# The first modulation by pairs of k-tiles, with three chunks of w_in beside it

## The chip, the cores and the metric

One core of a Trainium2 chip (trn2). The metric is the device time of one execution in microseconds; the times before are three runs of the same kernel.

## The reference, cut to what matters

Two transformer blocks on x of 256 tokens and 2048 channels, all in FP32. What the change touches is the start of the first block:

```python
mod = jax.nn.silu(c) @ w_ada[l] + b_ada[l]
shift1, scale1, gate1, shift2, scale2, gate2 = jnp.split(mod, N_MOD, axis=-1)
h = rms_norm(x, norm1_w[l]) * (1.0 + scale1[:, None]) + shift1[:, None]
proj = h @ w_in[l]
u_pool, q, k, v, g_a, g_b = jnp.split(proj, split_at, axis=-1)
```

c is one row of 2048, w_ada is 2048 x 12288, w_in is 2048 x 8192. Behind it come the pooling and the stick-breaking attention on u_pool, q, k and v, two up-projections under the gates g_a and g_b, w_o, the feed-forward (w_ff1, w_ff2), and a second pair of mixers (a: banded attention, b: compressed attention) with a final norm.

## The kernel before, in words

All five engines have a program written out by hand, in the order in which it runs; semaphores alone tie them together (`Marks`). TensorE multiplies 128 x 128 tiles of activations, turned (`act_a_high` and `act_a_low`, k-tile by k-tile), with chunks of 512 weight columns. Weights and activations are split into a high and a low part (fp32r), and a product is three matmuls (`mm_tile`, lines 571 to 573) for each of the two token tiles; so one k-tile of a chunk is six matmuls of 512 columns, and a chunk of 16 k-tiles is 96.

The weights come as a stream (`weight_stream`): SyncE (SP) loads units of four k-tiles, 1 MB each, into the ring `raw` of four (line 421); ScalarE (ACT) casts half a unit, two k-tiles, to `w_high` (1013), VectorE (DVE) makes `w_low` from the difference (1446), both three halves ahead of TensorE in rings of four. SP waits for the `w_low` of the unit that a load overwrites. Each chunk is finished before the next begins, in one of two pairs of PSUM banks. The order is "in" 0 to 7 (the first quarter, the fourth, the second, the third of the four parts of 1024, twice), "ga" and "ua" four times each in turn, "gb" and "ub" the same, "wo", and the rest.

Ahead of it stands a prologue. The shift and the scale of the first norm are 4096 columns of `c @ w_ada`. SP loads them as 32 pieces of four k-tiles by 512 columns into `raw` (404). Of the four k-tiles TensorE takes one as a product of a single row (615), DVE two as running sums in `ada_acc_vec` (1510, 1514), GpSimd (POOL) one in `ada_acc_pool` (463 to 468); the two sums are folded into the row by matmuls with ones (618, 620), ACT copies the row out of PSUM (1043), and TensorE turns it into columns (623). In the middle, after four of eight column groups, stand the transposes of the normalised x (582), copied by DVE (1524). When all columns are there, DVE makes `mod1` (1529, 1531), and ACT and DVE modulate and split two k-tiles at a time into `act_a_high` and `act_a_low` (1050, 1053, 1536).

The other 32 pieces of w_ada, of 256 columns, are spread over later chunks (`PIECES`): POOL loads them in ring buffers of two k-tiles (438), DVE sums 16 k-tiles, one instruction each (1464, 1467), TensorE adds up over the partitions (591, 599), DVE keeps the result. Eight pieces lie in "in", four in "ga", eight in "gb" and "ub", four in "wo", eight in "f1". In "ga" and "ua" DVE also works for the stick-breaking attention: at the start of each ga it copies `k_pair` and `v_pair` (1642, 1643), for which the scores on TensorE wait (697, at k = 2), and at the end of each ua it multiplies the gate in (1661). In chunk 1 of "in" DVE and POOL also make the counts and bands of the pooling; chunks 2, 3, 6 and 7 end with a normalisation of the heads on DVE (up to 1585).

Of the kernel before, what the change touches and what calls it, by code (L numbers as in the profile page):

```python
# [38 lines left out]
PRO = 2 * D // CH * (KT // UK)  # L39
# [7 lines left out]
                 "cols_made", "c_tanh", "x_squared", "xn_made", "row_copied", "xT_made", "ident_made"),  # L47
# [53 lines left out]
class Chunk:  # L101
    def __init__(self, w, row, col, nk, half, unit, pair, width, before, k0, whole):
        self.w, self.row, self.col, self.nk = w, row, col, nk
        self.k0, self.first, self.last = k0, k0 == 0, k0 + nk == whole
        self.half, self.unit, self.pair, self.width, self.before = half, unit, pair, width, before
        self.per = SK if width == CH else KT // 2
        self.halves = nk // self.per


def weight_stream(t):  # L110

    chunks, every = {}, []
    state = {"half": 0, "unit": 0}
    newest = {0: None, 1: None}

    def add(name, w, row, col, nk, pair, width=CH, k0=0, whole=None):
        c = Chunk(w, row, col, nk, state["half"], state["unit"], pair, width, newest[pair], k0, whole or nk)
        c.name = name
        state["half"] += c.halves
        state["unit"] += c.halves // 2  # L120
        newest[pair] = c
        chunks[name] = c
        every.append(c)

# [8 lines left out]
    for i in range(2):  # L133
        add(("in", 4 * i), w_in, 0, CH * i, KT, 0)
        add(("in", 4 * i + 1), w_in, 0, 3 * POOL_W + CH * i, KT, 1)
        add(("in", 4 * i + 2), w_in, 0, POOL_W + CH * i, KT, 0)
        add(("in", 4 * i + 3), w_in, 0, 2 * POOL_W + CH * i, KT, 1)
# [32 lines left out]
    return chunks, every, state["half"]  # L170
# [3 lines left out]
PIECES = ([(("in", n), 2 * D + AC * n) for n in range(8)]  # L174
          + [(("ga", n), 3 * D + AC * n) for n in range(4)]
          + [((("gb", "ub")[j], n), 3 * D + AC * (4 + 2 * n + j)) for n in range(4) for j in range(2)]
          + [(("wo", n), 3 * D + AC * (12 + n)) for n in range(4)]
          + [(("f1", i, 2 * j), 5 * D + AC * (2 * i + j)) for i in range(4) for j in range(2)])
PIECE_OF = {name: p for p, (name, _) in enumerate(PIECES)}

# [35 lines left out]
def body(nc, t, ctx, known):  # L216
    m = Marks(nc, ctx, known)
    landed, of = m.landed, m.of
    C, EVERY, HALVES = weight_stream(t)
# [5 lines left out]
    pair = [banks[:, 0:2, :], banks[:, 2:4, :]]  # L225
# [34 lines left out]
    acc_g = sb("ada_acc_pool", [P, 2, CH], 121984)  # L260
    row_s = sb("ada_row", [1, 2, CH], 126080)
# [167 lines left out]
    def pool_program(G):  # L429
# [24 lines left out]
        for w in range(PRO):  # L454
# [1653 lines left out]
```

## Time and profile before

| | |
|---|---|
| three runs | 2411.17, 2414.98, 2419.09 us (median 2414.98) |
| the profiled execution | 2406.36 us, span 2405.1 us, mean granted clock 0.969 |
| busy share of PE, PEld, DVE, ACT, POOL | 94%, 75%, 64%, 45%, 12% |
| chain that ended last | PE 86%, DVE 7%, DMA 2%, ACT 2%, issue 2% |
| DMA | 468.52 MB, mean 195 GB/s |

PE is TensorE at its matmuls, PEld at its weight loads, which overlap them. The span runs from the first to the last instruction of the profiled execution, and is 1.3 us shorter than its time. The chain is followed back from the last instruction through whatever released it; its shares say on which engine the time that sets the end was spent. Busy shares are means over stages that differ: the 40 slices of the page show PE at 5 and 7 tenths in the first two (120 us) and at 8 or 9 in almost all later ones. The granted clock is that of TensorE, 1.00 being 2.4 GHz and 0.50 being 1.2 GHz.

### The profile page before, as it was taken

To read this page: it belongs to the slowest core of one execution; us is meant where nothing else is said; L and a number is where in the kernel's file an instruction comes from. 1 tells how busy PE (TensorE), PEld (TensorE's weight loads), DVE (VectorE), ACT (ScalarE), POOL (GpSimd) and SP (SyncE) were. 2 spreads that over 40 slices of the span, in tenths; PEclk is the share of its full clock that TensorE was granted. 3 is DMA by queue.
4 is the path that set the end of the run, shared out by engine and by line. 5 is a ranking of instruction groups with operands and counts; after the bars stand their busy time and mean duration, and the time that the engine had idled before them with its cause. 6 is when DMAs were issued, how large, how long until landed. Compare 5 with 4: busy or idle time off the path is not lost.

```text
span 2405.1 us, 27296 instructions
## 1 busy us (share of the span) xinstructions
PE 2253.9 (94%) x10579; PEld 1803.2 (75%) x10579; DVE 1528.9 (64%) x2050; ACT 1084.0 (45%) x1566; POOL 297.4 (12%) x374
## 2 busy tenths in 40 slices
PE   5789999999898999999999998999998879999998
PEld 1267878877687888888888886788887767877776
DVE  6878778878877645645655655565654435676664
ACT  1054445643346543543543545555545413555543
POOL 6633221123322100100100000000000000000000
PEclk9899999999999999999999999999999989999999
DMA  9887856678877756756756654444446433333333
GB/s 333 291 282 267 279 182 220 214 226 276 265 251 244 231 192 211 237 192 208 236 187 215 222 175 158 158 141 149 149 145 205 136 110 123 123 99 112 106 123 123
DMA packets 225268, 468.52 MB, mean 195 GB/s; under 512 B 13850, under 2 KB 19188, under 8 KB 224500
## 3 DMA queue, kind: packets, MB, share of 16 engines
q1 hardware_dynamic: 196944, 388.78, 48.6%
q0 software_dynamic: 20480, 67.13, 8.6%
q10 hardware_dynamic: 7716, 10.88, 1.3%
q8 instruction: 84, 1.38, 0.2%
q14 instruction: 44, 0.36, 0.0%
HBM read 464.65 MB, written 2.10 MB: 194 GB/s over the span
## 4 chain that ended last, share of the span: by engine, by line
PE 86%; DVE 7%; DMA 2%; ACT 2%; issue 2%; POOL 0%; ACTq 0%; DVEq 0%
PE banks L571 25%; PE banks L573 24%; PE banks L572 24%; PE banks L582 2%; DVE ada_acc_vec L1514 2%; PE banks L832 2%; PE banks L844 1%; DMA ada_w<-in_w_ada 1%; DVE ada_acc L1467 1%; PE banks L858 1%; PE banks L859 1%; PE banks L857 1%; PE banks L922 1%; DMA raw<-in_w_ada 1%; DMA x<-in_x 0%
## 5 line engine op out<-in xcount | busy, mean ns | idle before, releaser
L1446 DVE TENSOR_TENSOR w_low<-raw,w_high 128x1024 fp32r<-128x1024 f32 x674 | 821.6, 1224 | 597.4 <-ACT w_high L1013 596.3
L1013 ACT CAST w_high<-raw 128x1024 fp32r<-128x1024 f32 x674 | 701.2, 1047 | 798.5 <-PE banks L573 797.7
L571 PE MATMUL banks<-w_high,act_a_high 128*128 128x512 f32 (+1 forms) x1696 | 686.5, 405 | 14.3 <-DVE w_low L1446 8.4
L573 PE MATMUL banks<-w_high,act_a_low 128*128 128x512 f32 (+1 forms) x1696 | 665.6, 392 | 0.0
L572 PE MATMUL banks<-w_low,act_a_high 128*128 128x512 f32 (+1 forms) x1696 | 664.6, 392 | 0.0
L571 PEld LDWEIGHTS banks<-w_high,act_a_high 128*128 128x128 f32 x1696 | 324.9, 192 | 92.4 <-issue 22.0
L573 PEld LDWEIGHTS banks<-w_high,act_a_low 128*128 128x128 f32 x1696 | 323.8, 191 | 69.2
L572 PEld LDWEIGHTS banks<-w_low,act_a_high 128*128 128x128 f32 x1696 | 325.0, 192 | 61.8
L438 POOL DMA_DIRECT2D ada_w<-in_w_ada x256 | 186.8, 730 | 953.4 <-DVE ada_acc L1467 947.2
L571 PE MATMUL banks<-w_high,act_b_high 128*128 128x512 f32 x640 | 250.6, 392 | 0.8 <-DVE act_b_low L1671 0.8
L573 PE MATMUL banks<-w_high,act_b_low 128*128 128x512 f32 x640 | 249.6, 390 | 0.0
L572 PE MATMUL banks<-w_low,act_b_high 128*128 128x512 f32 x640 | 249.6, 390 | 0.0
L1467 DVE SCALAR_TENSOR_TENSOR ada_acc<-ada_w,cT,ada_acc 128x256 f32<-128x256 f32 x480 | 231.8, 483 | 16.8 <-DMA ada_w<-in_w_ada 7.5
L571 PEld LDWEIGHTS banks<-w_high,act_b_high 128*128 128x128 f32 x640 | 120.5, 188 | 25.6 <-DVE act_b_low L1671 0.8
L573 PEld LDWEIGHTS banks<-w_high,act_b_low 128*128 128x128 f32 x640 | 120.6, 188 | 25.2
L572 PEld LDWEIGHTS banks<-w_low,act_b_high 128*128 128x128 f32 x640 | 120.6, 188 | 25.0
L443 POOL TENSOR_TENSOR inverse_rms<-sums_for_rms,minus_half 128x2 f32<-128x2 f32 (+1 forms) x9 | 10.4, 1152 | 976.5 <-DVE sums_for_rms L1485 976.5
L1317 ACT ACTIVATE scores<-scores,minus_max 128x128 f32<-128x128 f32 x192 | 85.1, 447 | 32.5 <-DVE minus_max L1856 30.7
L1514 DVE SCALAR_TENSOR_TENSOR ada_acc_vec<-raw,cT,ada_acc_vec 128x512 f32<-128x512 f32 x56 | 75.2, 1343 | 7.7 <-DMA raw<-in_w_ada 4.4
L1328 ACT COPY ada_w<-banks 128x768 f32<-128x768 f32 x48 | 38.3, 799 | 57.6 <-PE banks L844 57.4
L615 PE MATMUL banks<-raw,cT 128*1 128x512 f32 x64 | 40.2, 762 | 18.4 <-DMA raw<-in_w_ada 13.7
L571 PE MATMUL banks<-w_high,act_d_high 128*128 128x512 f32 x128 | 51.4, 401 | 1.6 <-DVE act_d_low L1671 1.6
(336 smaller groups left out, 2213.9 us busy)
## 6 DMA issues: line engine op xcount, KB each, us to landing
raw<-in_w_ff SPq DMA_DIRECT2D x128, 1024.0 KB, 5.2
raw<-in_w_in SPq DMA_DIRECT2D x64, 1024.0 KB, 6.6
ada_w<-in_w_ada POOLq DMA_DIRECT2D x256, 256.0 KB, 5.0
raw<-in_b_w_in SPq DMA_DIRECT2D x44, 1024.0 KB, 5.0
raw<-in_a_w_in SPq DMA_DIRECT2D x36, 1024.0 KB, 5.1
raw<-in_w_ada SPq DMA_DIRECT2D x32, 1024.0 KB, 7.2
raw<-in_w_o SPq DMA_DIRECT2D x16, 1024.0 KB, 7.3
raw<-in_a_w_out SPq DMA_DIRECT2D x16, 1024.0 KB, 5.2
```

The costliest lines, as they stand in the source:

```text
L438: G.dma_start(ada_w[:, u % ADA_RING, :, :], t["w_ada"][0, q * AK * P:(q + 1) * AK * P, col:col + AC] .rearrange("(k p) n -> p k n", p=P)). ...
L571: T.matmul(out, xh, wh, start=(c.first and k == 0), stop=False)
L572: T.matmul(out, xh, wl, start=False, stop=False)
L573: last = T.matmul(out, xl, wh, start=False, stop=(c.last and k == c.nk - 1))
L582: tr = T.transpose(bank(b)[:, j * SEQ + tt * P:j * SEQ + (tt + 1) * P], src[:, tt, c0 + j * P:c0 + (j + 1) * P], ident[:, :])
L615: T.matmul(row, cT[:, u * UK:u * UK + 1], raw[:, w % RAW, 0, :], start=(u == 0), stop=False).then_inc(*done("pro_pe", w))
L832: mm = T.matmul(bank(e)[:, c0:c0 + n], qG[o:o + HD, i % 4, tt * P:(tt + 1) * P], k_[o:o + HD, 0:n], start=True, stop=True)
L1013: A.copy(WH[:, h % SPL, :, :], split_ap(h)).then_inc(*done("high", h))
L1317: A.activation(sc[:, s, c0:c0 + n], sc[:, s, c0:c0 + n], ACT.Exp, scale=R, bias=nm[:, i // 4, j, tt:tt + 1], accum_out=sm[:, i // 4, j, tt ...
L1446: V.tensor_tensor(WL[:, h % SPL, :, :], split_ap(h), WH[:, h % SPL, :, :].bitcast(F32), ALU.subtract).then_inc(*done("low", h))
L1467: V.scalar_tensor_tensor(out=acc_, in0=w, scalar=c, in1=acc_, op0=ALU.mult, op1=ALU.add).then_inc(*done("ada_acc", (p, a)))
L1514: V.scalar_tensor_tensor(out=acc_v[:, n, :], in0=r[:, kk, :], scalar=cT[:, k + kk:k + kk + 1], in1=acc_v[:, n, :], op0=ALU.mult, op1=ALU.a ...
```

## The change

The modulation of the first norm is made for two k-tiles of the activations at a time, by eight rounds. A round loads the 256 columns of the shift and the 256 of the scale that belong to two k-tiles: four loads of four k-tiles of w_ada, each as two DMAs, into four buffers `ada_first` of their own. Of each buffer DVE sums two k-tiles in `ada_acc_vec`, TensorE takes the other two (half and half) with the weights of w_ada as the stationary operand and one column of c as the moving one, which gives columns at once: 8 matmuls in the program for a buffer, and 4 more that fold in DVE's sum. POOL does none of it. The transposes of x stand after the first round's sums, and their copies are shared between ACT and DVE.

Between the sum groups of the next round stand the matmuls of three chunks of w_in, ("in", 0) to ("in", 2), two k-tiles of each; a third pair of PSUM banks serves the third chunk. Units and halves of these chunks are taken in turn, and SP issues their loads in groups of three between those of w_ada. The pieces of w_ada that lay in "in" 0 to 2 have moved: "in" 3 to 7 take five, each "ua" takes one, "wo" three. The sum over the partitions of a piece always lies in the next chunk (`DUE_STEP`) and in one PSUM bank. The counts and bands of the pooling are made in chunk 3.

```diff
@@ weight_stream
+    cols = [CH * i + part * POOL_W for i in range(2) for part in (0, 3, 1, 2)]
+    early = [define(("in", n), w_in, 0, cols[n], KT, n) for n in range(EARLY)]
+    for i in range(KT // UK):
+        for c in early:
+            take_unit(c, i)
+        for sub in range(2):
+            for c in early:
+                take_half(c, c.units[i], sub)
...
+PLACES = ([("in", n) for n in range(EARLY, 8)] + [(name, n) for n in range(4) for name in ("ga", "ua")]
+          + [(name, n) for n in range(4) for name in ("gb", "ub")] + [("wo", n) for n in range(3)])
+DUE_STEP = {"in": 4, "ga": 5, "ua": 6, "gb": 4, "ub": 4, "wo": 4, "f1": 4}
@@ sync_program
+        def first_load(i, u):
+            if i > 0:
+                S.wait_ge(*of("first_pe", (i - 1, u)))
+                S.wait_ge(*of("first_vec", (i - 1, u, 1)))
+            for m_ in range(2):
+                S.dma_start(first[u][:, :, m_, :], first_w[:, u * UK:(u + 1) * UK, m_, i * AC:(i + 1) * AC]).then_inc(*landed(f"first_landed{u}", i))
...
+        for i in range(KT // 2):
+            for u in range(FIRST_RING):
+                if i % 2 == 0 and u == (2 if i else FIRST_RING):
+                    for n in range(EARLY):
+                        unit_load(i // 2 * EARLY + n)
+                first_load(i, u)
+            if i == 0:
+                for n in range(EARLY):
+                    unit_load(n)
@@ tensor_program
+        def first_pe(i, u):
+            T.wait_ge(*of(f"first_landed{u}", i))
...
+            for kk in (UK - 2, UK - 1):
+                for j in range(4):
+                    mm = T.matmul(sum_cols(i)[:, j:j + 1], first[u][:, kk, j // 2, j % 2 * P:(j % 2 + 1) * P],
+                                  cT[:, u * UK + kk:u * UK + kk + 1], start=(u == 0 and kk == UK - 2 and j == 0), stop=False)
+            mm.then_inc(*done("first_pe", (i, u)))
...
+        for i in range(KT // 2):
+            more = i + 1 < KT // 2
+            for n in range(EARLY):
+                if more:
+                    first_pe(i + 1, n)
+                if n == 0:
+                    T.wait_ge(*of("a_low", ("in", i)))
...
+                for k in (2 * i, 2 * i + 1):
+                    mm_tile(C["in", n], k, STAT["in"])
+            if more:
+                first_pe(i + 1, FIRST_RING - 1)
+                first_sum(i + 1)
@@ vector_program
+        for i in range(KT // 2):
+            more = i + 1 < KT // 2
+            for n in range(EARLY):
+                if more:
+                    first_vec(i + 1, n)
+                if n == 0:
+                    modulate("in", 2 * i, tmp0)
+                    if i == 0:
+                        for h in range(AHEAD):
+                            rest(h)
+                rest(EARLY * i + n + AHEAD)
+            if more:
+                first_vec(i + 1, FIRST_RING - 1)
+                first_mod(i + 1)
...
             for k in range(8):
                 rests(C["ua", n], k)
+                ada_tiles(C["ua", n], k)
+                ada_keep(C["ua", n], k)
```

What PE does in a round stands in its own order of the changed kernel; L638 is a sum group with the weights of w_ada, L645 folds in DVE's sum, and L595 to L597 are the three matmuls of `mm_tile` (each block goes on with nine more like them).

```order
L638 MATMUL banks<-cT,ada_first_77 128x1 [waits columns_vector,first_landed0]
L638 MATMUL banks<-cT,ada_first_77 128x1 x7
L595 MATMUL banks<-w_high,act_a_high 128x512 [waits low_vector,a_low_vector]
...
L638 MATMUL banks<-cT,ada_first_78 128x1 [waits first_landed1]
L638 MATMUL banks<-cT,ada_first_78 128x1 x7
L595 MATMUL banks<-w_high,act_a_high 128x512 [waits low_vector]
...
L638 MATMUL banks<-cT,ada_first_80 128x1 [waits first_landed3]
L638 MATMUL banks<-cT,ada_first_80 128x1 x7
L645 MATMUL banks<-ones,ada_acc_vec 128x1 [waits first_vec_vector]
L645 MATMUL banks<-ones,ada_acc_vec 128x1 x3
```

Before, no matmul of w_in stood on PE ahead of the last column of the modulation; now each block of 12 has a sum group ahead of it, and a round ends with two groups and the fold.

The second place is DVE at the end of the first ua, before the change (1446 is w_low, 1661 the gate, 1642 and 1643 the copies for the next ga):

```order
L1612 TENSOR_SCALAR merged<-merged 128x2x512 [waits pair_scalar]
L1446 TENSOR_TENSOR w_low<-raw,w_high 128x1024 [waits high_scalar] x4
L1661 TENSOR_TENSOR merged<-banks,merged 128x2x512 [waits pair_vector,used_tensor]
L1476 COPY mod_62<-banks 128x2 [waits ada_summed_tensor]
L1642 COPY k_pair<-kT 128x512 [waits stick_tensor]
L1643 COPY v_pair<-values 128x512
```

and of the changed kernel, the same stretch without its middle (1482 is w_low, 1500 and 1503 the sums of a piece of w_ada):

```order
L1666 TENSOR_SCALAR merged<-merged 128x2x512 [waits pair_scalar]
L1482 TENSOR_TENSOR w_low<-raw,w_high 128x1024 [waits high_scalar]
L1500 TENSOR_SCALAR ada_acc<-ada_w,cT 128x256 [waits ada_summed_tensor,ada_landed0]
L1503 SCALAR_TENSOR_TENSOR ada_acc<-ada_w,cT,ada_acc 128x256 [waits ada_acc_vector]
L1503 SCALAR_TENSOR_TENSOR ada_acc<-ada_w,cT,ada_acc 128x256 [waits ada_acc_vector,ada_landed1]
L1503 SCALAR_TENSOR_TENSOR ada_acc<-ada_w,cT,ada_acc 128x256 [waits ada_acc_vector]
L1482 TENSOR_TENSOR w_low<-raw,w_high 128x1024 [waits high_scalar]
...
L1503 SCALAR_TENSOR_TENSOR ada_acc<-ada_w,cT,ada_acc 128x256 [waits ada_acc_vector,ada_landed3]
L1503 SCALAR_TENSOR_TENSOR ada_acc<-ada_w,cT,ada_acc 128x256 [waits ada_acc_vector]
L1718 TENSOR_TENSOR merged<-banks,merged 128x2x512 [waits pair_vector,used_tensor]
L1696 COPY k_pair<-kT 128x512 [waits stick_tensor]
L1697 COPY v_pair<-values 128x512
```

Sixteen sums of a piece have come between the four w_low, all ahead of the gate and the copies.

## Rows read from the trace of the kernel before

**Rows 1.** Windows of the trace; share of DMA engines and GB/s at the right.

```profile
core 0: us, PE busy (x) PEld busy (x) DVE busy (x) ACT busy (x) POOL busy (x), PEclk, DMA share, GB/s
20.00:40.00 20.00, 15.12 (x26) 3.16 (x25) 18.66 (x13) 2.35 (x2) 18.38 (x13) 1.00 0.84 294
...
38.60:45.40 6.80, 5.75 (x18) 1.39 (x16) 4.16 (x4) 0.58 (x1) 2.41 (x4) 1.00 1.03 380
...
80.00:100.00 20.00, 12.16 (x24) 3.08 (x24) 17.58 (x16) 0.93 (x2) 10.80 (x8) 0.74 0.91 319
...
132.80:137.50 4.70, 4.64 (x11) 3.70 (x12) 4.58 (x6) 3.11 (x5) 0.00 (x0) 0.50 1.04 341
```

**Rows 2.** Timeline: start us, us, engine, line; first block matmul, and a cast.

```profile
132.86 0.76 PE L571 MATMUL banks<-w_high,act_a_high 128*128 128x512 f32 x1 [7.12 <-DVE w_low L1446]
...
171.28 1.05 ACT L1013 CAST w_high<-raw 128x1024 fp32r<-128x1024 f32 x1 [1.67 <-PE banks L573]
```

**Rows 3.** Timeline: ACT takes chunks 1 and 2, end of a normalisation on DVE.

```profile
179.68 1.02 ACT L1086 COPY values<-banks 128x1024 f32<-128x1024 f32 x1 [1.91 <-PE banks L573]
...
204.61 1.03 ACT L1091 ACTIVATE qn<-banks 128x1024 f32<-128x1024 f32 x1 [1.61 <-PE banks L573]
...
208.89 1.23 DVE L1585 TENSOR_TENSOR qn<-banks,inverse_rms 128x1024 f32<-128x1024 f32 x1 [1.79 <-POOL inverse_rms L443]
```

**Rows 4.** Timeline of PE: third piece of w_ada, transposes of xn.

```profile
19.31 1.86 PE L615 MATMUL banks<-raw,cT 128*1 128x512 f32 x2 [3.20 <-DMA raw<-in_w_ada]
...
69.63 3.54 PE L582 MATMUL banks<-ident,xn 128*128 128x128 f32 x16 [0.63 <-DVE cols L1521]
...
74.84 1.25 PE L582 MATMUL banks<-ident,xn 128*128 128x128 f32 x8 [0.19 <-DVE xT L1524]
```

**Rows 5.** Timeline of the weight loads (PEld), eight at each clock.

```profile
57.98 1.78 PEld L623 LDWEIGHTS banks<-ones,ada_row 1*128 1x128 f32 x8 [2.45 <-ACT ada_row L1043]
...
41.99 0.96 PEld L623 LDWEIGHTS banks<-ones,ada_row 1*128 1x128 f32 x8 [1.60 <-ACT ada_row L1043]
```

**Rows 6.** Timeline: from the last row turned to the first pair split.

```profile
124.69 1.05 PE L623 MATMUL banks<-ones,ada_row 1*128 1x1 f32 x8 [0.67 <-ACT ada_row L1043]
...
126.27 1.09 ACT L1050 ACTIVATE tmp<-xT,mod 128x256 f32<-128x256 f32 x2 [1.63 <-DVE mod L1531]
...
128.04 0.69 DVE L1536 TENSOR_TENSOR act_a_low<-tmp,act_a_high 128x512 fp32r<-128x512 f32 x1 [1.87 <-ACT act_a_high L1053]
```

**Rows 7.** L1514, the sums of 512 columns on DVE; ns min/median/max.

```profile
L1514 DVE SCALAR_TENSOR_TENSOR ada_acc_vec<-raw,cT,ada_acc_vec x56: 750/1376/1643, 17.3 to 120.5; 128x512 f32<-128x512 f32 x56
```

**Rows 8.** Windows of the trace in mixer b, the chunk of 96 columns.

```profile
1936.40:1939.80 3.40, 3.40 (x31) 3.28 (x29) 1.83 (x7) 2.02 (x3) 0.00 (x0) 1.00 0.62 238
...
1946.70:1950.00 3.30, 3.30 (x17) 3.30 (x17) 0.00 (x0) 0.00 (x0) 0.00 (x0) 0.50 0.02 5
```

**Rows 9.** Window of one period of ga and ua.

```profile
378.40:417.80 39.40, 39.40 (x178) 32.75 (x178) 32.66 (x48) 23.19 (x28) 5.78 (x8) 1.00 0.64 214
```

**Rows 10.** Timeline of DVE and PE around ga and ua.

```profile
385.76 0.69 DVE L1622 TENSOR_TENSOR log_beta<-log_beta,z_log 128x512 f32<-128x512 f32 x1 [0.95 <-ACT z_log L1112]
...
410.92 1.22 DVE L1446 TENSOR_TENSOR w_low<-raw,w_high 128x1024 fp32r<-128x1024 f32 x1
...
419.20 0.42 DVE L1643 COPY v_pair<-values 128x512 f32<-128x512 f32 x1
...
420.68 0.59 PE L697 MATMUL banks<-qT,k_pair 128*128 128x256 f32 x2
```

**Rows 11.** DVE in the first ub (timeline), and its waits, 500 to 660 us.

```profile
527.49 1.23 DVE L1446 TENSOR_TENSOR w_low<-raw,w_high 128x1024 fp32r<-128x1024 f32 x1 [0.24 <-ACT w_high L1013]
...
542.76 1.22 DVE L1690 TENSOR_TENSOR qT<-banks,qT 128x1024 f32<-128x1024 f32 x1
...
DVE ada_acc L1467 <- DMA ada_w<-in_w_ada: 6.8, 4, 2.7
```

**Rows 12.** Waits of PE, 500 to 660 us.

```profile
PE banks L571 <- DVE y_b_low L1665: 4.0, 1, 4.0
```

More of the change, by code:

```diff
@@ L123, in add @@
         every.append(c)
+        return c
+    def add(*args, **more):
+        c = define(*args, **more)
+        for i in range(c.nk // c.per // 2):
+            take_unit(c, i)
+            for sub in range(2):
+                take_half(c, c.units[i], sub)
     def add_outputs(name, w):
@@ L422, in sync_program @@
+        for i in range(KT // 2):
[7 more added lines that the diff above has]
+                    unit_load(n)
+        for u in range(EARLY * (KT // UK), len(UNITS)):
+            unit_load(u)
         for tt in range(NT):
@@ L512, in pool_program @@
             chunk_loads(("ub", n))
-        for n in range(4):
+        for n in range(3):
             chunk_loads(("wo", n))
@@ new lines, in first_sum @@
+        def first_sum(i):
+            T.wait_ge(*of("first_vec", (i, FIRST_RING - 1, 1)))
+            for j in range(4):
+                mm = T.matmul(sum_cols(i)[:, j:j + 1], acc_v[:, i % 2, j * P:(j + 1) * P], ones[:, 0:1],
+                              start=False, stop=(j == 3))
+            mm.then_inc(*done("first_summed", i))
+        emptied[0] = of("c_cols")
+        first_pe(0, 0)
+        first_pe(0, 1)
+        T.wait_ge(*of("small_landed", "rows2"))
+        T.transpose(bank(3)[:, 0:P], rows1[:, :], ident[:, :])
@@ L1069, in heads_store, with first_modulate, in_take @@
                              scale=cols2[:, at[norm]:at[norm] + 1]).then_inc(*done("heads_stored", (n, half)))
-        for n in range(8):
+        def first_modulate(i):
+            A.wait_ge(*of("mod1_made", i))
+            A.wait_ge(*of("xT_made", i))
+            modulate("in", 2 * i, xT[:, 2 * i:2 * i + 2, :], mod1, AH, tmp0)
+        def in_take(n):
+            c = C["in", n]
+            A.wait_ge(*ready(c))
+            if n % 4 == 0:
+                A.copy(u_sb[:, :, CH * (n // 4):CH * (n // 4 + 1)], pair[c.pair]).then_inc(*done("pair_free", c.name))
+            elif n % 4 == 1:
+                if n == 1:
+                    A.wait_ge(*of("a_low", ("in", KT // 2 - 1)))
+                A.copy(vv[:, :, CH * (n // 4):CH * (n // 4 + 1)], pair[c.pair]).then_inc(*done("pair_free", c.name))
+            else:
+                if n > 2:
+                    A.wait_ge(*of("heads_turned", (n - 1 if n % 4 == 3 else n - 3, 1)))
+                A.activation(qn[:, :, :], pair[c.pair], ACT.Square).then_inc(*done("heads_squared", n))
+        first_modulate(0)
+        for h in range(AHEAD):
+            cast(h)
+        for i in range(KT // 2):
+            for n in range(EARLY):
+                cast(EARLY * i + n + AHEAD)
+                if i == KT // 2 - 1 and n > 0:
+                    in_take(n - 1)
+            if i + 1 < KT // 2:
+                first_modulate(i + 1)
+        in_take(EARLY - 1)
+        A.dma_start(wp, t["w_pool"][0].rearrange("g (a q) e -> q (g a) e", q=P)).then_inc(*landed("pool_w_landed"))
+        for n in range(EARLY, 8):
             c = C["in", n]
```

427 lines of the change are left out of this document (179 added, 248 removed).

## The prediction, made before the changed kernel was run

> **What bounds the kernel now.** Read the shares in the table first: TensorE (PE) is busy 94% of a span of 2405.1 us and is 86% of the chain that ended last, so nearly everywhere the end moves with PE's own time. Then the stretches of the opening [rows 1]: in them PE is busy for 12 to 15 of 20 us, mostly with products of a single row that serve the modulation, at a mean granted clock of 0.74 to 1.00. The first block matmul starts only at 132.86 us [rows 2]; TensorE has then still the whole w_in to do. ScalarE (ACT) takes the sums of chunk ("in", 1) at 179.68 and of ("in", 2) at 204.61 us [rows 3]. So I judge the change by two times: when chunk 2 is done, and what the rest costs after it.
>
> **Part 1: the opening up to the first block.** The same bytes arrive in the same order as before (x and four 1 MB pieces of w_ada), so I take the landings of before; the third was used at 19.31 us [rows 4], the fourth landed while its group was at work. A sum group is 8 matmuls in the program, and each FP32 matmul is two weight loads in the trace, so 16 loads; eight such loads took 1.78 us at the lower clock and 0.96 at the upper [rows 5], so a group is 3.6 or 1.9 us. Groups 3 and 4: 19.3 + 3.6 + 3.6 = 26.5; the closing group of 8 loads 1.8, so 28.3. The transposes of xn took 6.5 us (69.63 to 76.1) [rows 4]: 34.8. Then modulation of a pair on ACT (1.09 and the cast), the difference on VectorE (DVE) 0.69 [rows 6], the first w_low 1.2 behind it: **the first block starts at 39 us** instead of 132.9. I cost the splitting of the loads at nothing here, since PE waits for its own groups more than for them.
>
> **Part 2: the eight rounds.** A round has three blocks of 12 matmuls (two k-tiles of each of three chunks), four sum groups and a closing group, all in one row on PE (the first order piece above). A block takes 2.72 us at the upper clock, a cast and its wait for the next, 1.05 + 1.67 [rows 2]. After the closing group PE can start no block until mod1 is added, the pair modulated and split: from the end of L623 (125.74) to the end of act_a_low (128.73) that took 3.0 us [rows 6], and the first group of the next round lies in it. So a round at the upper clock is 3.0 + 3 x 2.72 + 3 x 1.9 + 1.0 = 17.9 us. DVE needs 8 sums of 512 columns at 0.75, the shortest of L1514, when POOL no longer works beside it [rows 7], 0.7 and 3 x 1.22, in all 10.5 us: hidden under PE. ACT needs 3 x 1.05 + 1.7. The DMA brings 4 MiB of w_ada a round and 3 MiB of w_in every second one: 49.3 MB with x and the bias. The busiest stretch shows 380 GB/s, the slowest of those that DMA fills 294 [rows 1], so all of it lies between 130 and 168 us, under the 185 us at which the last round starts; it would bind only where rounds are shorter than they are here.
>
> What decides is the clock. From the third block to the next round's first lie 1.9 + 1.0 + 3.0 = 5.9 us in which PE does nothing but weight loads with one column behind each. The trace has a stretch like it: from 1936.4 us on PE runs loads with 96 columns each (the gates of mixer b) without a gap, first at 1.00, and from 1946.7 us the granted clock reads 0.50 while PE is busy 3.30 of 3.30 us [rows 8]. One column is less than 96, so I expect the clock to fall to 1.2 GHz once in each round, inside that stretch, and to come back in the first block: from 132.8 us dense blocks ran 4.7 us at 0.50 [rows 1], which costs 2.35 us. Another 0.5 us for loads that fall into the lower clock. Between blocks 1, 2 and 3 only one group lies (1.9 us), and I take the clock to stay. Round: 17.9 + 2.35 + 0.5 = **20.8 us**. Seven rounds and the blocks of the eighth: 39 + 7 x 20.8 + 8.2 + 2.35 = 195 us for the end of chunk 2, against 204.6: **9 us gained**. Ends: 173 us with all at the upper clock, 275 with all at the lower (3.6 + 3 x 5.1 + 3 x 3.6 + 1.8 = 31.5 a round).
> By the Trainium skill (TensorE: Matmul & The Clock Gate, "Why this matters for your kernels") it is idle gaps of PE between bursts that cost the upper clock, and here PE would be idle for only about 1.1 us a round, so by that page the clock would stay and the first rival hold; the matmuls of 96 columns speak against it.
>
> **Part 3: chunk 3.** The counts and bands, which lay in chunk 1, now lie in chunk 3, right behind the normalisation of chunk 2 and before that of chunk 3. PE lost about 3 us to what they had put off: 179.68 to 204.61 is 24.9 for 16 k-tiles, where 8 x 2.72 = 21.8. A normalisation keeps DVE 5.5 us from ACT's squares at 204.61 to the end of L1585 at 210.1 [rows 3], and one now lies on either side. I put **3 us** lost (0 to 6).
>
> **Part 4: ga and ua.** There were 24 pieces of w_ada before the feed-forward, 8 in "in"; now "in" takes 5, and the four "ua" chunks take one each (the second order piece). This is the term I trust most. A period of ga and ua lasts 39.4 us, and DVE is busy 32.66 of it [rows 9]. The added piece is 16 instructions at 0.48, about 7.5 us: 40.2, before any wait. And it stands between the w_low of ua and L1661, behind which k_pair and v_pair are copied, for which PE waits at k = 2 of the next ga (L697 at 420.68; the copies end at 419.6, 1.1 us before) [rows 10]. The "ub" chunk has the very sequence: from 527.49 to 542.76, where L1690 starts, 15.3 us, 2.7 of them for a landing of ada_w; the four such waits of the stage are 6.8 us in all [rows 11]. From 410.92 (first w_low of ua) that block now ends not at 417.67 but 12.5 us (no landing wait) to 14.2 (the mean of 1.7) later, at 423.4 to 425.1; L1661 and the copies, 2.0 us; PE would have come at 420.7. The first stall is 4.7 to 6.4 us. In later periods DVE no longer waits for ACT's logarithm (twice 0.95 [rows 10]) nor for a few casts (0.5), so its period is 30.7 (419.6 less 39.4, to 410.92) - 2.4 + 12.5 or 14.2 + 2.0 = 42.8 to 44.5: 3.4 to 5.1 us, twice. At the end y_b_low is late by another 4 to 6, on top of the 4.0 us that PE waits for it already [rows 12]. Sum 16 to 23 us, **20 taken**, since the landing waits came in each of the four ub. The clock lost in these stalls costs nothing extra, DVE being the slower.
>
> **Part 5: the rest.** wo has three pieces instead of four, f1 adds its sums at k = 4 instead of 12; DVE has room there and PE waits for neither: 0. POOL is free until the last round and starts its loads of ada_w only then, ahead of chunk 3 by some 15 us: 0. The row copies on ACT and POOL's accumulator go: they lay in the opening already counted.
>
> **Sum.** -9 + 3 + 20 = +14 us, 2420 against the profiled execution's 2406.4. The median of the runs is 2415.0, 8.6 above that execution; I add the 14 to it: **2429 us**. A measurement of this kernel can tell about 0.3%, 7 us, from no change.
>
> **The rivals.**
> B, the clock stays at 2.4 GHz: chunk 2 ends at 39 + 7 x 17.9 + 8.2 = 173 us, 32 gained, and -32 + 3 + 20 = -9: 2406 us, faster. It decides from rounds under 19 us on. For it: PE does not pause there. Against it: [rows 8]. Chance 0.15.
> C, the clock falls in each gap between blocks too: 17.9 + 3 x 2.35 + 1.5 = 26.5 a round, 240 us for chunk 2, +35 + 3 + 20 = +58: 2473 us; at the lower clock throughout 2508. For it: a mean of 0.74 in an opening whose PE was busy 12 of 20 us [rows 1]. Against it: there PE paused, while from the first block to the third it does not, and dense blocks are most of that time. Chance 0.20.
> D, DVE takes the ua pieces into its idle time (6.7 us of each 39.4) and the stage costs 5 us: -9 + 3 + 5, 2414 us, same. For it: DVE has 6.7 idle and 7.5 come. Against it: 3.3 of the idle time are waits for ACT in the middle of a chain, and the place is the worst one. Chance 0.15.
> The forecast has 0.50; its own range is 2418 to 2440.
>
> **How the numbers follow.** Faster: B's greater part, and the edges of D and of the forecast, 0.18. Same: the rest of B, most of D, the forecast's low end, 0.22. Slower: 0.60. The range begins at 2402 (B with the lower end of part 4) and ends at 2468, which leaves out most of C and little else.
>
> **What would show it.** In the profile after: first block at 39 us; eight rounds of about 21 us; granted clock at 0.50 for some 5 to 8 us of each round, about 0.7 to 0.8 in the mean; chunk 2 taken at about 195 us; PE idle before L697's counterpart for 3 to 6 us in each ga from the second on, released by the pair copies on DVE, and DVE over 95% busy in ga and ua. If the mean clock of the rounds is 0.95 or more, B holds; if a round takes 26 us, C. If PE does not wait for k_pair, part 4 is wrong.

## The result, and the profile after

| | before | after |
|---|---|---|
| median of the runs on one chip | 2413.07 us (2408.37 to 2419.09) | 2444.07 us (2441.02 to 2453.50) |
| ratio, 95% interval | | 1.0139 (1.0115 to 1.0163) |
| profiled execution, mean granted clock | 2406.36 us, 0.969 | 2453.50 us, 0.955 |
| first block matmul | 132.86 us | 40.78 us |
| ACT takes chunk 2, chunk 4 | 204.61, 250.77 | 193.43, 251.50 |
| ga(1), ga(2), ga(3), gb(0) begin | 378.4, 417.8, 457.3, 500.8 | 382.8, 430.8, 479.5, 536.5 |
| xn of the feed-forward begins | 757.1 | 798.3 |

The change costs 31 us of median where 14 were forecast: slower as predicted, inside the range, by twice the size. The profiled execution after is itself 9 us above its median, and that of before lay below its own, so the two traces differ by 47 us; which stage loses is read from the traces, how much in all from the medians. What one pair of traces shows is compared with the traces of the other runs where it can be.

The opening is as forecast. Windows of the trace after: two stretches of 20 us in the rounds, then the end of one round and the first block of the next.

```profile
core 0: us, PE busy (x) PEld busy (x) DVE busy (x) ACT busy (x) POOL busy (x), PEclk, DMA share, GB/s
...
60.00:80.00 20.00, 18.89 (x108) 16.64 (x108) 10.10 (x14) 4.67 (x7) 0.00 (x0) 0.84 0.95 307
80.00:100.00 20.00, 19.14 (x108) 16.86 (x108) 9.79 (x15) 4.44 (x7) 0.00 (x0) 0.84 0.78 267
...
76.20:79.60 3.40, 2.69 (x25) 2.60 (x24) 1.77 (x5) 2.03 (x4) 0.00 (x0) 0.90 0.68 215
79.80:85.60 5.80, 5.54 (x14) 4.40 (x15) 2.84 (x4) 0.42 (x1) 0.00 (x0) 0.50 0.70 227
```

The timeline between them, PE, DVE and ACT:

```profile
76.07 1.03 PE L645 MATMUL banks<-ones,ada_acc_vec 128*128 128x1 f32 x8
76.97 1.93 PE L638 MATMUL banks<-cT,ada_first 128*128 128x1 f32 x16
...
77.54 1.09 ACT L1077 ACTIVATE tmp<-xT,mod 128x256 f32<-128x256 f32 x2 [6.42 <-DVE mod L1560]
...
79.31 0.69 DVE L1581 TENSOR_TENSOR act_a_low<-tmp,act_a_high 128x512 fp32r<-128x512 f32 x1 [0.61 <-ACT act_a_high L1080]
80.06 0.80 PE L595 MATMUL banks<-w_high,act_a_high 128*128 128x512 f32 x1 [1.17 <-DVE act_a_low L1581]
```

Rounds last 20.1 to 20.5 us (the folds begin at 56.00, 76.07, 96.37 and so on to 178.08). The fold, the sum group and the 1.17 us of waiting are followed by a first block wholly at 1.2 GHz (0.50): 12 matmuls in 5.3 us instead of 2.7.

What follows is not as forecast. ACT takes chunks 2, 3 and 4 (timeline after; the last line is chunk 4 before), and PE's waits in chunks 3 and 4:

```profile
193.43 1.03 ACT L1107 ACTIVATE qn<-banks 128x1024 f32<-128x1024 f32 x1 [0.70 <-PE banks L597]
...
220.20 1.03 ACT L1107 ACTIVATE qn<-banks 128x1024 f32<-128x1024 f32 x1 [3.85 <-PE banks L597]
...
251.50 1.02 ACT L1099 COPY merged<-banks 128x1024 f32<-128x1024 f32 x1 [1.61 <-PE banks L597]
...
250.77 1.02 ACT L1082 COPY merged<-banks 128x1024 f32<-128x1024 f32 x1 [1.61 <-PE banks L573]
```

```profile
212.18 0.50 PE L595 MATMUL banks<-w_high,act_a_high 128*128 128x512 f32 x1 [1.15 <-DVE w_low L1482]
...
217.15 0.50 PE L595 MATMUL banks<-w_high,act_a_high 128*128 128x512 f32 x1 [1.93 <-DVE w_low L1482]
...
224.12 0.50 PE L595 MATMUL banks<-w_high,act_a_high 128*128 128x512 f32 x1 [1.24 <-DVE w_low L1482]
...
228.03 0.70 PE L621 MATMUL banks<-ada_acc,ones 128*128 128x256 f32 x2 [0.88 <-DVE ada_acc L1503]
232.37 1.86 PE L606 MATMUL banks<-ident,qn 128*128 128x128 f32 x8 [3.64 <-DVE qn L1621]
```

From chunk 2 to chunk 4 it takes 58.1 us, where before it took 46.2 (from 204.61 [rows 3] to 250.77): the 11.2 us won in the rounds are gone by the end of chunk 4. PE idles 8.8 us in five places, all for DVE, and behind the last of them the clock stood at 0.50 for 3.4 us.

In ga and ua: the waits of PE and of DVE (365 to 705 us) and two windows, the second a whole period:

```profile
PE banks L732 <- DVE v_pair L1697: 18.4, 3, 7.0
PE banks L606 <- DVE qT L1746: 15.5, 4, 8.1
...
DVE ada_acc L1503 <- DMA ada_w<-in_w_ada: 12.6, 8, 2.3
DVE log_beta L1676 <- ACT z_log L1148: 10.7, 6, 2.5
...
PE banks L595 <- DVE y_b_low L1721: 9.3, 1, 9.3
```

```profile
417.70:430.80 13.10, 13.10 (x59) 10.90 (x58) 11.72 (x19) 7.01 (x9) 4.02 (x6) 1.00 0.71 230
...
430.80:479.50 48.70, 41.66 (x182) 34.37 (x182) 40.36 (x65) 23.41 (x27) 11.91 (x17) 0.93 0.68 221
```

Against [rows 9] a period has 9.3 us more; DVE is busy 40.36 us of it, 7.7 more, which is the added piece. It is not over 95% busy, as I had said it would be, but 83%. The three periods of the table grew by 8.6, 9.2 and 13.5 us, 31.3 in all, of which 5.3 is the longer wait for y_b_low at the end (9.3 us for 4.0 [rows 12]).

### The profile page after: what moved, and what is told of

Read it like the earlier page. It is cut to its first block, busy times and chain, and to the rows that moved or that the text cites. A ratio compares the mean times of both kernels' runs of the same rounds, so it can differ in the third digit from the quotient of the medians.

```text
span 2451.9 us, 28078 instructions
## 1 busy us (share of the span) xinstructions
PE 2296.1 (94%) x10995; PEld 1888.1 (77%) x10995; DVE 1491.2 (61%) x2061; ACT 1082.3 (44%) x1562; POOL 218.9 (9%) x318
## 4 chain that ended last, share of the span: by engine, by line
PE 76%; issue 10%; DVE 7%; DMA 3%; ACT 2%; POOL 1%; ACTq 0%; SPq 0%; DVEq 0%; POOLq 0%
PE banks L595 22%; PE banks L597 22%; PE banks L596 22%; PE banks L606 2%; DMA ada_w<-in_w_ada 2%; DVE ada_acc L1503 2%; PE banks L861 2%; PE banks L873 1%; PE banks L888 1%; PE banks L887 1%; PE banks L886 1%; PE banks L951 1%; DMA ada_first<-in_w_ada 1%; DVE w_low L1482 1%; ACT w_high L1043 1%
## 5 line engine op out<-in xcount | busy, mean ns | idle before, releaser
L595 PE MATMUL banks<-w_high,act_a_high 128*128 128x512 f32 (+1 forms) x1696 | 700.3, 413 | 27.4 <-DVE act_a_low L1581 9.7
L597 PE MATMUL banks<-w_high,act_a_low 128*128 128x512 f32 (+1 forms) x1696 | 676.4, 399 | 0.0
L596 PE MATMUL banks<-w_low,act_a_high 128*128 128x512 f32 (+1 forms) x1696 | 675.9, 399 | 0.0
L595 PEld LDWEIGHTS banks<-w_high,act_a_high 128*128 128x128 f32 x1696 | 331.8, 196 | 109.0 <-issue 17.4
L597 PEld LDWEIGHTS banks<-w_high,act_a_low 128*128 128x128 f32 x1696 | 330.8, 195 | 72.1
L596 PEld LDWEIGHTS banks<-w_low,act_a_high 128*128 128x128 f32 x1696 | 332.2, 196 | 63.6
L595 PE MATMUL banks<-w_high,act_b_high 128*128 128x512 f32 x640 | 251.2, 392 | 1.4 <-DVE act_b_low L1727 1.4
L597 PE MATMUL banks<-w_high,act_b_low 128*128 128x512 f32 x640 | 250.1, 391 | 0.0
L595 PEld LDWEIGHTS banks<-w_high,act_b_high 128*128 128x128 f32 x640 | 120.8, 189 | 26.5 <-DVE act_b_low L1727 1.8
L597 PEld LDWEIGHTS banks<-w_high,act_b_low 128*128 128x128 f32 x640 | 120.8, 189 | 25.5
L483 POOL TENSOR_TENSOR inverse_rms<-sums_for_rms,minus_half 128x2 f32<-128x2 f32 (+1 forms) x9 | 10.6, 1178 | 1163.8 <-DVE sums_for_rms L1525 1163.8
L1353 ACT ACTIVATE scores<-scores,minus_max 128x128 f32<-128x128 f32 x192 | 85.1, 446 | 31.4 <-DVE minus_max L1903 30.7
L638 PEld LDWEIGHTS banks<-cT,ada_first 128*128 128x128 f32 x512 | 70.4, 215 | 12.3 <-issue 8.0
L638 PE MATMUL banks<-cT,ada_first 128*128 128x1 f32 x512 | 67.9, 263 | 9.8 <-DMA ada_first<-in_w_ada 9.8
L595 PE MATMUL banks<-w_high,act_d_high 128*128 128x512 f32 x128 | 51.3, 401 | 1.6 <-DVE act_d_low L1727 1.6
```

Of the source, the lines that this page charges most:

```text
L595: T.matmul(out, xh, wh, start=(c.first and k == 0), stop=False)
L596: T.matmul(out, xh, wl, start=False, stop=False)
L597: last = T.matmul(out, xl, wh, start=False, stop=(c.last and k == c.nk - 1))
L638: mm = T.matmul(sum_cols(i)[:, j:j + 1], first[u][:, kk, j // 2, j % 2 * P:(j % 2 + 1) * P], cT[:, u * UK + kk:u * UK + kk + 1], start=(u ...
L1353: A.activation(sc[:, s, c0:c0 + n], sc[:, s, c0:c0 + n], ACT.Exp, scale=R, bias=nm[:, i // 4, j, tt:tt + 1], accum_out=sm[:, i // 4, j, tt ...
```

## The experiments

All ratios are against the kernel before, on the same chip; gains are told against the changed kernel's 2444.07 us (ratio 1.0139) unless said otherwise. The runs were made on several chips, on which the kernel before had medians of 2410.0 to 2413.1 us, so a gain in these medians is good to some 3 us; the ratios are the safer comparison.

### The ua pieces left out

```diff
-PLACES = ([("in", n) for n in range(EARLY, 8)] + [(name, n) for n in range(4) for name in ("ga", "ua")]
+PLACES = ([("in", n) for n in range(EARLY, 8)] + [(name, n) for n in range(4) for name in ("ga",)]
...
-            if 8 <= p < 24:
+            if 8 <= p < 20:
```

> The four pieces of w_ada in ua are left out with their loads, sums and folds; the modulation of the feed-forward lacks its last four pieces (1024 columns of the scale, taken as zero ahead of the one that is added), so the output is not the reference's. All else is as in the changed kernel. Theory A: the whole excess of ga and ua is theirs; the three periods fall back to 39.4, 39.4 and 43.6 us, and the kernel is faster by 31 us (27 to 35). Theory B: a part of it comes from the sums that now lie in the next chunk (DUE_STEP) and from the loads of ada_w behind them: 10 us or more stay, and it is faster by 15 to 22.

Measured: 2414.98 us, ratio 1.001 (0.9995 to 1.0026), 29 us gained, 31 by the ratios. A window of it as long as a period; y_b_low is awaited 4.3 us again:

```profile
413.40:452.80 39.40, 39.40 (x176) 32.75 (x176) 32.99 (x47) 23.27 (x28) 5.79 (x8) 1.00 0.63 214
```

The scores of one ga and of the next stand 39.3 us apart, where before it was 39.4. So theory A: the pieces in ua are worth 29 to 31 us, not the 20 I had taken, and everything else in the change comes out at about zero.

### Order or load in ga and ua

k_pair ahead of ua's sums:

```diff
-            V.tensor_copy(kS[:, :, :], kT[:, h0:h0 + 2, :])
+            if n == 0:
+                V.tensor_copy(kS[:, :, :], kT[:, h0:h0 + 2, :]).then_inc(*done("pair_copied", (n, "k")))
...
             gate(C["ga", n], m_)
+            if n < 3:
+                V.wait_ge(*of("sb_scored", (n, 1)))
+                V.tensor_copy(kS[:, :, :], kT[:, h0 + 2:h0 + 4, :]).then_inc(*done("pair_copied", (n + 1, "k")))
             for k in range(8):
```

> The copy k_pair for the next ga is taken ahead of the sums of the piece in ua (v_pair stays where it is); the pieces stay in ua. Theory A (order): TensorE waits 18.4 us in three ga for the copies, and the lower clock behind each wait costs some 3 us more; both go, and only DVE's own load is left, 40.4 us busy in 48.7, so a period falls from 48.4 to 42 to 44 us and the kernel is faster by 13 us (9 to 18). Theory B (throughput): DVE has too much to do in a period, the wait comes back at the w_low or at the suffix sums, and at most 4 us are gained.

Measured: 2435.93 us, ratio 1.0101 (1.0072 to 1.013): 8 us gained, 9 by the ratios, at the edge of A's 9 to 18 and over B's 4. PE's waits from 365 to 705 us:

```profile
PE banks L595 <- DVE y_b_low L1726: 10.1, 1, 10.1
PE banks L740 <- DVE log_beta L1686: 5.7, 3, 1.9
PE banks L595 <- DVE w_low L1483: 2.8, 3, 1.1
PE banks L740 <- DVE log_rest L1682: 2.1, 3, 0.9
```

The 18.4 us at k_pair are gone, 10.6 stand elsewhere (beside y_b_low, whose wait is 10.1 for 9.3), and the period is 44 us. Both theories hold a part: some 4 us of a period were the order, the 4.6 us left (44.0 against 39.4) are DVE's load. In the run with all three orders, below, a 44.0 us period shows DVE busy for 40.12.

The wait for y_b_low moved to its user:

```diff
-        T.wait_ge(*of("y_b_low"))
         for n in range(4):
...
+            if n == 0:
+                T.wait_ge(*of("y_b_low"))
             for k in range(8):
                 ada_sum(C["ub", n], k)
```

> TensorE waits for y_b_low ahead of the first gb, 9.3 us of idle time, though only the first ub uses it; here the wait stands at the first ub. Nothing else changes. Theory A (a wait in the wrong place): DVE catches up while gb is multiplied, and the kernel is faster by 9 us and some 1 to 3 of clock, 8 to 12. Theory B (DVE is behind and stays so): the w_low that stand behind y_b_low in DVE's queue are as late, the wait comes back at L595 on w_low, and less than 4 us is gained.

Measured: 2436.19 us, ratio 1.0109 (1.0077 to 1.014), 8 us gained, the low end of A. DVE makes the time up: from 500 to 710 us PE waits for w_low only once more, 1.0 us. The same move in the kernel before:

> The kernel before, with the wait for y_b_low moved from the first gb to the first ub, the one repair among these that the kernel before can have as well. It waits 4.0 us there. If the wait is just in the wrong place, 4 us faster (3 to 5); if DVE hands it on, nothing.

Measured: 2405.3 us, ratio 0.9974 (0.9956 to 0.9991), 6 us gained for a wait of 4.0. The interval allows 2 to 11. So this is a fault that the change made larger, not one that it made.

### The bands elsewhere

```diff
+BANDS = 4
...
-            chunk_loads(("in", n), bands=n == EARLY)
+            chunk_loads(("in", n), bands=n == BANDS)
...
-            if n == EARLY:
+            if n == BANDS:
                 V.wait_ge(*of("pool_fill", "count"))
```

> The counts and bands of the pooling are made in chunk 4 instead of chunk 3 (nothing else changes). Theory A (crowding): in the changed kernel DVE has in chunk 3 the sixteen sums of a piece, four counts, four bands, eight w_low and a normalisation on either side, so its w_low come late and chunk 4 is taken at 251.5 us, 35.0 after chunk 3's end where 23.1 would do. Chunk 4 has a normalisation only at its start; then the loss falls from 12 us to about 3, chunk 4 is taken at about 243, and the kernel is faster by 8 us (6 to 11). Theory B (the bands cost what they cost wherever they stand, or the loss comes from the handing over from the rounds): the loss only moves, and the time stays within 3 us.

Measured: 2445.21 us, ratio 1.0133 (1.0098 to 1.0168). The time says nothing (2436.0 to 2448.8); in the trace chunk 2 is taken at 194.8 and chunk 4 at 244.7, 49.9 us where it was 58.1, of which chunk 5 gives back 2.7. Repeated on top of the three orders, with more runs:

> The three orders, and the bands in chunk 4 (pieces as in the changed kernel). The bands alone gave nothing in the time of the changed kernel (1 us slower, with 12 us between its fastest and slowest run) and 4 us in its trace up to the first ga. Theory A: the crowding of chunk 3 costs what the trace says; 4 us faster than the three orders alone, 2407 to 2409. Theory B: what it gives there is lost later; 2412, no difference.

Measured: 2405.89 us, ratio 0.9978 (0.9963 to 0.9994), 6 us under the three orders alone (1.0006, 0.9988 to 1.0024, below). Theory A, if only just: the two intervals overlap by a little.

### The clock in the rounds

A fill of four matmuls behind the first sum group:

```diff
+                if n == 0 and more:
+                    for _ in range(FILL):
+                        T.matmul(banks[:, 6 + (i + 1) % 2, SEQ:2 * SEQ], ident[:, :], xT[:, 0, :], start=False, stop=False)
                 if n == 0:
                     T.wait_ge(*of("a_low", ("in", i)))
```

> Four more matmuls of 256 FP32 columns stand in each round between the first sum group of the next round and the first block, in which TensorE waits 1.2 us for act_a_low; their result goes to unused columns and is read by nobody. Theory A (clock): the stretch of weight loads with one column each lets the clock fall and the first block pays for it at 0.50; with columns in the stretch the granted clock stays at 1.00, a round falls from 20.5 to about 18.7 to 19.5 us (the matmuls themselves outlast the wait by about 1 us), and the kernel is faster by 7 to 13 us. Theory B: the clock falls all the same, the fill only lengthens the round by 1 to 2 us, and the kernel is slower by 7 to 14 us.

Measured: 2446.21 us, ratio 1.0142 (1.0112 to 1.0172): neither. The clock still fell in each round, for 3.4 and 6.8 us in turn instead of always 6.8, and the fill itself (up to 3.7 us at the lower clock) ate that up: rounds of 19.7 and 21.4 us in turn. It stood too late: the fold and a sum group lay ahead of it, and in the round shown by its timeline from 73.95 us the clock had fallen at 74.91, 3.3 us before the fill began.

The fold ahead of the third block, so that the modulation runs under it:

```diff
+                if more and n == EARLY - 1:
+                    first_pe(i + 1, FIRST_RING - 1)
+                    first_sum(i + 1)
...
-            if more:
-                first_pe(i + 1, FIRST_RING - 1)
-                first_sum(i + 1)
+            if i + 2 < KT // 2:
+                first_pe(i + 2, 0)
```

> In each round the last sum group and the fold stand ahead of the third block instead of behind it (on DVE the sums and mod1 too, and the pair's difference ahead of the next round's first sums), so that the modulation of the next pair is made under the third block. Theory A (TensorE's order binds the rounds): the wait for act_a_low (9.7 us over seven rounds) goes, no more than two sum groups and the fold stand between dense blocks, 4.8 us, and the clock may stay at 1.00; a round falls from 20.5 to 17 us with the clock up, or to 19 where it still falls, and the kernel is faster by 10 to 25 us. Theory B (the DMA is next behind it): the rounds move 6.2 MB each and the busiest 20 us of them show 311 GB/s at a DMA share of 0.92; then no round gets under 19.3 us whatever the clock, waits for ada_first or raw appear on TensorE, and at most 9 us are gained.

Measured: 2432.16 us, ratio 1.0082 (1.0055 to 1.011): 12 us gained, 14 by the ratios, chunk 2 taken at 179.0 instead of 193.4. Windows: a stretch of 20 us, the two groups and the fold, and the block behind them:

```profile
80.00:100.00 20.00, 20.00 (x112) 17.74 (x111) 10.34 (x15) 4.85 (x6) 0.00 (x0) 0.83 0.99 340
85.40:88.90 3.50, 3.50 (x34) 3.50 (x33) 0.98 (x2) 1.04 (x1) 0.00 (x0) 1.00 1.07 363
88.90:95.30 6.40, 6.40 (x21) 5.34 (x21) 3.30 (x6) 1.71 (x3) 0.00 (x0) 0.51 1.05 389
```

PE is busy for all of the 20 us and the clock falls all the same, from the fold on. It fell behind each of the seven folds, for 3.4 us behind four and 6.8 behind three. Theory B is refuted: rounds of 17.9 us occur (folds at 53.05, 70.94, 88.81) where it allowed none under 19.3, and the DMA moves 340 GB/s over 20 us where I had taken 311 for its most. The Trainium skill (DMA: Bandwidth & Descriptors, "Specifications") gives some 358 GB/s as a core's share of the HBM; these 340, and 352 over 20 us in the run with all together, come near it, while the window of 6.4 us above, with 389, lies over it.

Groups 2 and 3 apart, on top of that:

```diff
                 for k in (2 * i, 2 * i + 1):
                     mm_tile(C["in", n], k, STAT["in"])
+                    if more and n == 1 and k == 2 * i:
+                        first_pe(i + 1, 2)
```

> On top of the kernel with the fold ahead of the third block: the second block of a round is cut into its two k-tiles and the third sum group stands between them, so that no more than one group and the fold (2.9 us) lie between dense matmuls, where it was two and the fold (4.7 us). In the run before TensorE never waited in the rounds and the granted clock still fell to 0.50 in each, for 3.4 or 6.8 us from the fold on. Theory A (the length of the stretch with one column per load is what lets the clock fall): it stays at 1.00, a round needs 17 us of TensorE, and the DMA, then at 0.95 to 1.00, holds it at about 18.3; chunk 2 is taken 2 to 6 us earlier than at 179.0. Theory B (the share of such loads in a whole round does it): the clock falls as before, and nothing changes (within 2 us).

Measured: 2425.63 us, ratio 1.0064 (1.0044 to 1.0083), 18 us under the changed kernel, 6.5 under the run before; chunk 2 taken at 170.2. Windows:

```profile
80.00:100.00 20.00, 20.00 (x134) 18.12 (x133) 11.82 (x16) 5.90 (x7) 0.00 (x0) 1.00 0.98 336
100.00:120.00 20.00, 20.00 (x125) 17.79 (x123) 12.02 (x18) 4.85 (x6) 0.00 (x0) 0.91 0.98 312
120.00:140.00 20.00, 18.95 (x125) 16.80 (x124) 10.54 (x15) 4.97 (x7) 0.00 (x0) 1.00 1.04 340
```

The clock falls behind three of the seven folds, for 3.4 us each, and behind the other four not at all; a round without a fall lasts 16.3 or 16.4 us, 17.7 where PE waited, and one with a fall 17.9. That is A for the clock, if not in every round. That the DMA would hold a round at 18.3 was wrong again; it does make PE wait once, in the window from 120 us.

### Together

The three orders (fold ahead, k_pair first, y_b_low at ub), nothing left out:

> The order of the rounds, of k_pair and of the wait for y_b_low, each as in its own experiment, together in the changed kernel; the same work throughout. If the three add up: 8 for k_pair, 8 to 10 for y_b_low and 5 to 20 for the rounds below the changed kernel, 2405 to 2423 us, about the kernel before. If DVE is what binds ga and ua, the two of them overlap: after k_pair the wait for y_b_low was still 10.1 us, so they should add up, and less than 12 for both together speaks for DVE.

Measured: 2412.18 us, ratio 1.0006 (0.9988 to 1.0024). 32 us gained, where the three alone gave 8, 8 and 12, 28 in sum: they add up, and level the changed kernel with the one before.

The pieces of w_ada dealt out tile by tile, on top of the orders and the bands:

```diff
+SHARE = {'in': [16, 10, 22, 18, 18], 'ga': [19, 19, 19, 19], 'ua': [0, 0, 0, 0], 'gb': [16, 16, 16, 16], 'ub': [16, 16, 16, 16], 'wo': [24, 24, 24, 16]}
...
+            if c.name + (k,) in TILES:
+                for p, a in TILES[c.name + (k,)]:
+                    ada_tile(p, a)
```

> The three orders (rounds with the fold ahead, k_pair first, y_b_low awaited at ub), the bands in chunk 4, and the 24 pieces of w_ada dealt out tile by tile: none in ua, 16, 10, 22, 18, 18 tiles in chunks 3 to 7, 8 in the pooling, 19 in each ga, 16 in each gb and ub, 24, 24, 24 and 16 in wo. Nothing is left out. Theory A: DVE has room for the four pieces of ua elsewhere (18.4 of 22 us busy in wo, 16.8 of 22 in chunks 5 and 6, 10.5 of 23 in the pooling); the period of ga and ua falls from 44.0 to 40 us, 12 us over three, 4 come from the bands, and the time is 2393 to 2398 us, 0.6% under the kernel before. Theory B: DVE has no room anywhere, the waits only move into wo and the chunks; within 5 us of the three orders, 2408 to 2416.

Measured: 2401.88 us, ratio 0.9968 (0.9954 to 0.9982): 10 us under the three orders, 4 under those with the bands moved, which is within the noise of the two (0.9954 to 0.9982 and 0.9963 to 0.9994). Between A and B. With the groups apart and the partition sums later:

> The pieces dealt out as before this, and the sum groups of the rounds apart; the sums over the partitions come seven steps behind a piece's last tile instead of four (TensorE waited 13.0 us for ada_acc), ga has 18 tiles each, wo 24, 24, 24 and 20. If the gains add up: 8 us for the groups apart, 8 to 11 for the later sums, from 2401.9 to 2383 to 2388 us, 1% under the kernel before. If DVE is full in wo, the waits for ada_acc become waits for w_low, and it is 2392 to 2396.

Measured: 2394.17 us, ratio 0.9924 (0.9897 to 0.9952): **the fastest of all, 0.8% under the kernel before**, though short of the 2383 to 2388 of full gains and inside the 2392 to 2396 that I had given for a DVE that is full in wo. Windows: a chunk of wo with 24 tiles, and a period of ga and ua:

```profile
685.30:713.70 28.40, 24.83 (x99) 19.93 (x98) 22.35 (x37) 11.52 (x14) 8.63 (x12) 0.88 0.79 264
386.10:425.80 39.70, 39.70 (x176) 32.76 (x175) 33.85 (x49) 23.11 (x29) 6.57 (x9) 1.00 0.67 219
```

The period is 39.7 us, as wanted, and in gb(1) it stands 31.5 us ahead of the kernel before; at the feed-forward 12.8. Most of the difference, 15 us, is lost between the last ub and the feed-forward. The third chunk of wo takes 28.4 us where one before took 23.1: PE waits in it 3.6 us for w_low, and in the fourth 4.8 us for ada_acc, and the clock falls behind both. Room in a mean (18.4 of 22 us) was not room in the place. A table with fewer tiles in wo was not tried.

## Why the prediction was right, and where it failed

**Right.** Part 1: the first block at 40.8 us (39). Part 2: rounds of 20.1 to 20.5 us (20.8), the clock at 0.50 for 6.8 us of each (5 to 8), 0.83 to 0.84 in the mean (I had said 0.7 to 0.8), chunk 2 at 193.4 (195), so -11 for -9. Rival B (clock stays) and C (falls in every gap) are out. [Rows 8] carried this: PE busy without a pause, narrow columns, and the clock down. By the Trainium skill (TensorE: Matmul & The Clock Gate, "Why this matters for your kernels") idle gaps cost the clock; the window of the fold-ahead run, with 20.00 of 20.00 us busy and a mean of 0.83, differs, and the measurement decides. The mechanism of part 4 was right too: PE waits in each later ga for the pair copies, 5.7, 7.0 and 5.7 us, released by DVE; rival D is out.

**Failed: the size of part 4, first term.** I forecast 16 to 23 us and took 20; leaving the pieces out gave 29. The forecast had a first stall of 4.7 to 6.4 us, then twice 3.4 to 5.1, then 4 to 6 for y_b_low; the trace has 8.6, 9.2, 8.2 and 5.3, so the term for y_b_low held and those of the periods did not. The step is this: "In later periods DVE no longer waits for ACT's logarithm (twice 0.95 ...) nor for a few casts (0.5), so its period is 30.7 (...) - 2.4 + 12.5 or 14.2 + 2.0". DVE from one copy to the next (timeline after):

```profile
440.20 0.42 DVE L1697 COPY v_pair<-values 128x512 f32<-128x512 f32 x1
...
446.15 0.69 DVE L1676 TENSOR_TENSOR log_beta<-log_beta,z_log 128x512 f32<-128x512 f32 x1 [1.49 <-ACT z_log L1148]
...
453.08 0.69 DVE L1676 TENSOR_TENSOR log_beta<-log_beta,z_log 128x512 f32<-128x512 f32 x1 [1.74 <-ACT z_log L1148]
...
472.18 1.22 DVE L1482 TENSOR_TENSOR w_low<-raw,w_high 128x1024 fp32r<-128x1024 f32 x1
...
480.86 2.11 DVE L1503 SCALAR_TENSOR_TENSOR ada_acc<-ada_w,cT,ada_acc 128x256 f32<-128x256 f32 x4 [1.27 <-DMA ada_w<-in_w_ada]
...
487.52 0.42 DVE L1697 COPY v_pair<-values 128x512 f32<-128x512 f32 x1
488.08 2.04 PE L732 MATMUL banks<-qT,k_pair 128*128 128x256 f32 x4 [5.71 <-DVE v_pair L1697]
```

From the end of the copies to the first w_low of ua: 31.6 us, where I had 28.3; from there to the end of the copies 15.8, where I had 14.5 to 16.2. So the block was sized well and the way to it was not. The logarithm's waits did not vanish, they grew from 1.9 to 3.2 us. A late engine no longer waits for others only if they run ahead; here PE was waiting for that very copy, so PE (its scores), ACT (its logarithm) and DVE set out together each time, one behind the other. In the same breath I wrote that the lower clock behind a stall costs nothing since DVE is slower. It stood at 0.50 for 6.8 us from 389.5, 437.3 and 485.1 us, and PE's scores, for which ACT and DVE wait, lie in it: the first of the three periods grew by 8.6 us, 5.7 of them the wait. In the second PE idles 7.0 us and is busy 2.3 us longer for the same work (41.66 against the 39.40 of [rows 9]), at a clock of 0.93: that is all of its 9.3. So the clock had a price on PE, which the forecast put at nothing; how much of DVE's longer way comes from the clock and how much from the chain was not measured by itself.

**Failed: part 3.** "A normalisation keeps DVE 5.5 us ..., and one now lies on either side. I put 3 us lost (0 to 6)": measured 11.9 from chunk 2 to chunk 4. I had carried over the 3 us that the counts and bands cost in chunk 1, where three halves of w_low were in hand and no normalisation stood near. DVE's order in chunk 3 adds four reciprocals of 1.75 us and their bands to eight w_low, sixteen sums and two normalisations. Of PE's 8.8 us of waiting, 4.3 are for late w_low (twice in chunk 3, once in chunk 4), 0.9 for the piece's sums, and 3.6 for the normalised heads of chunk 3, with the fall of the clock behind them. Moved by one chunk, counts and bands cost 6 us less; the other half is not explained run by run.

**Part 5's zero held, as far as can be told.** From gb(0) to the feed-forward the trace after takes 261.8 us and that of before 256.3. But four other traces with the ua pieces and the wait for y_b_low in place (bands in 4, k_pair first, the fill, groups apart) take 252.9 to 257.0 us, and a fifth (fold ahead) 259.3. So the 5.5 us are more likely the one execution's that was profiled than the change's. The same goes for 3.7 us between chunk 7 and ga(1): there the clock fell to 0.50 twice for 3.4 us after the change and not in the profile of before; but it did in the kernel before with only the wait for y_b_low moved, which is the same program up to there. Eight transposes at 324 us, in the kernel before and in that one:

```profile
323.87 1.09 PE L582 MATMUL banks<-ident,qn 128*128 128x128 f32 x8 [3.43 <-DVE qn L1585]
```

```profile
324.32 1.97 PE L582 MATMUL banks<-ident,qn 128*128 128x128 f32 x8 [3.42 <-DVE qn L1586]
```

The last 6 us of difference between the two profiled executions lie behind the start of the feed-forward: 1648.0 and 1648.6 us in the two traces of the kernel before, 1649.4 to 1655.5 in the twelve others. Part of that may be the change's; it stays open.

With the measured sizes the sum is -11 (part 2) + 12 (part 3) + 29 (ua, with what follows from it) = +30, or +32 with the 31 that the traces show for ga and ua, against 31 in the medians. That the time fell inside the stated range owes something to its width: it had been drawn wide for the clock, which came out as forecast, and took in errors of some 9 us each in parts 3 and 4, which the rivals did not cover.

## What to carry to other kernels

Work displaced from one stage has to be costed in the very place where it lands: who waits for the instruction behind it, and whether that one then waits in turn. When A makes B late and B's other inputs come from A's waiter, take no wait of B off the bill. And a share of busy time tells that there is room in a stage, not where: 16 sums in each ua cost 29 us, some 8 of them only by standing ahead of a copy. With the orders mended, the sum groups apart and the same sums spread about, the changed kernel ran 0.8% under the old one, which by moving one wait would itself be 0.3% faster.

## What the hardware showed that I had not expected

- The granted clock fell to 0.50 in stretches in which TensorE was never idle: two sum groups and the fold, 4.5 us of weight loads with one column behind each (67.45 to 71.97, for one; window 85.40 to 88.90, then 0.51). It fell behind all seven folds in each of the four traces with that order, and behind all seven of the changed kernel, where two groups, the fold and a wait make 5.7 us. With one group and the fold, some 2.8 us, between dense blocks it fell behind three of seven, and behind four of seven in the run with all together.
- The same wait costs more or less by whether the clock falls behind it, and two executions of the same program can differ in that: 3.43 and 3.42 us of waiting at 324 us, eight transposes in 1.09 us with the clock up and in 1.97 with it down, and the next wait, 1.95 us in both, again with the clock up in the one and down in the other. A single profile so carries several us of its own.
- 340 GB/s into SBUF over 20 us from SP's queue, in DMAs of 512 KB and 1 MB, with TensorE busy throughout.
